# Expert stage: output summed in PSUM, next tokens gathered before the last up product, scatter in fp32r, weights split over three lanes

## The reference, cut to what matters

```python
def moe_swiglu(h, w_router, b_router, w_gate, w_up, w_down):
    B, S, D = h.shape
    ht = h.reshape(B * S, D)
    logits = (ht @ w_router).astype(jnp.float32) + b_router.astype(jnp.float32)
    top_v, top_i = lax.top_k(logits, TOP_K)
    probs = jax.nn.softmax(top_v, axis=-1)
    gates = jnp.sum(jax.nn.one_hot(top_i, N_EXPERTS, dtype=jnp.float32) * probs[..., None], axis=1)
    out = jnp.zeros((B * S, D), jnp.float32)
    for e in range(N_EXPERTS):
        a = jax.nn.silu(ht @ w_gate[e]) * (ht @ w_up[e])
        out = out + gates[:, e:e + 1] * (a @ w_down[e]).astype(jnp.float32)
    return out.astype(h.dtype).reshape(B, S, D)
```

## Time and profile before

| | |
|---|---|
| median of 3 runs | 1954.76 us (1951.22 to 1954.91) |
| the profiled execution | 1952.92 us, span 1951.0 us |
| mean granted TensorE clock | 0.972 |
| TensorE products, busy | 1840.3 us, 94% of the span |
| VectorE, busy | 1479.4 us, 76% |
| ScalarE, busy | 1105.0 us, 57% |
| bytes moved | 484.29 MB, mean 248 GB/s |

### The profile page before, as it was taken

How to read it: one execution, slowest core, us unless ns; L and a number is a source line. 1 busy time by engine, 2 the same in 40 slices (tenths; PEclk the granted TensorE clock), 3 DMA queues, 4 the chain that set the end, 5 groups by cost and what they waited for, 6 DMA issues and landing times.

```text
span 1951.0 us, 24059 instructions
## 1 busy us (share of the span) xinstructions
PE 1840.3 (94%) x8694; PEld 1519.7 (78%) x8694; DVE 1479.4 (76%) x1327; ACT 1105.0 (57%) x980; POOL 32.2 (2%) x31
## 2 busy tenths in 40 slices
PE   6999998999799999979999989989999999899898
PEld 6788886888688888767877868868778778688686
DVE  5756576455666656758979979979889799798897
ACT  3345554433334466426766757767667667576574
POOL 0001000000000200000000000000000000000000
PEclk8999999999989999979999999999999999999999
DMA  5444355554225434537979979979989899799794
GB/s 221 153 171 151 108 173 215 186 186 151 103 102 203 149 129 136 178 140 262 376 288 348 374 249 366 374 251 376 327 301 374 290 333 374 270 358 374 264 373 172
DMA packets 243931, 484.29 MB, mean 248 GB/s; under 512 B 7472, under 2 KB 11824, under 8 KB 243760
## 3 DMA queue, kind: packets, MB, share of 16 engines
q1 hardware_dynamic: 243888, 483.70, 69.1%
HBM read 482.62 MB, written 1.05 MB: 248 GB/s over the span
## 4 chain that ended last, share of the span: by engine, by line
PE 84%; DVE 7%; ACT 4%; issue 3%; DMA 1%; DVEq 0%; POOL 0%; ACTq 0%; SPq 0%; POOLq 0%
PE ps L477 26%; PE ps L478 25%; PE ps L479 25%; PE ps L482 5%; PE ps L486 3%; DVE sb_wlo L295 2%; ACT sb_whi L288 2%; DVE sb_hlo L1222 1%; DVE sb_x L1700 1%; ACT sb_hhi L1133 1%; DMA sb_ringa<-in_w_in_dram 0%; DVE sb_z L1701 0%; DVE sb_w L1205 0%; DVE sb_hlo L1221 0%; ACT sb_w L910 0%
## 5 line engine op out<-in xcount | busy, mean ns | idle before, releaser
L295 DVE TENSOR_TENSOR sb_wlo<-sb_z,sb_whi 128x2048 fp32r<-128x2048 f32 (+1 forms) x372 | 843.9, 2271 | 195.2 <-ACT sb_whi L288 191.7
L288 ACT ACTIVATE sb_whi<-sb_z 128x2048 fp32r<-128x2048 f32 (+1 forms) x372 | 706.1, 1906 | 278.4 <-PE ps L479 278.4
L477 PE MATMUL ps<-sb_whi,sb_hhi 128*128 128x512 f32 (+1 forms) x1744 | 698.8, 401 | 57.4 <-DVE sb_hlo L1222 26.9
L478 PE MATMUL ps<-sb_whi,sb_hlo 128*128 128x512 f32 (+1 forms) x1744 | 683.4, 392 | 0.0
L479 PE MATMUL ps<-sb_wlo,sb_hhi 128*128 128x512 f32 (+1 forms) x1744 | 682.8, 391 | 0.0
L477 PEld LDWEIGHTS ps<-sb_whi,sb_hhi 128*128 128x128 f32 x1744 | 334.1, 192 | 138.7 <-issue 35.6
L479 PEld LDWEIGHTS ps<-sb_wlo,sb_hhi 128*128 128x128 f32 x1744 | 333.9, 191 | 70.4
L478 PEld LDWEIGHTS ps<-sb_whi,sb_hlo 128*128 128x128 f32 x1744 | 334.2, 192 | 66.1 <-issue 1.9
L295 DVE TENSOR_TENSOR sb_wlo<-sb_ringa,sb_whi 128x2048 fp32r<-128x2048 f32 (+1 forms) x90 | 200.9, 2240 | 85.6 <-ACT sb_whi L288 85.0
L288 ACT ACTIVATE sb_whi<-sb_ringa 128x2048 fp32r<-128x2048 f32 (+1 forms) x90 | 168.5, 1877 | 155.5 <-DMA sb_ringa<-in_w_in_dram 78.8
L477 PE MATMUL ps<-sb_whi,sb_ahi 128*128 128x512 f32 x568 | 222.2, 391 | 1.0 <-DVE sb_alo L1221 1.0
(11 more groups left out here) (201 smaller groups left out, 1027.0 us busy)
## 6 DMA issues: line engine op xcount, KB each, us to landing
sb_z<-in_moe_w_gate_dram SPq DMA_DIRECT2D x112, 1024.0 KB, 5.9
sb_z<-in_moe_w_up_dram SPq DMA_DIRECT2D x112, 1024.0 KB, 6.1
sb_z<-in_moe_w_down_dram SPq DMA_DIRECT2D x112, 1024.0 KB, 5.6
sb_ringa<-in_w_in_dram SPq DMA_DIRECT2D x68, 1024.0 KB, 4.8
sb_z<-in_ffn_w_gate_dram SPq DMA_DIRECT2D x10, 1024.0 KB, 5.3
sb_z<-in_ffn_w_up_dram SPq DMA_DIRECT2D x10, 1024.0 KB, 6.4
sb_z<-in_ffn_w_down_dram SPq DMA_DIRECT2D x10, 1024.0 KB, 4.8
sb_ringa<-in_w_out_dram SPq DMA_DIRECT2D x8, 1024.0 KB, 4.9
```

What stands on the lines that cost most here:

```text
L288: nc.scalar.activation(whi[:, lane(layer, phase, s), 0:n], raw_slot(layer, phase, s)[:, 0:n], ACT.Copy).then_inc(hi_done, 1)
L295: nc.vector.tensor_tensor(wlo[:, k, 0:n], raw_slot(layer, phase, s)[:, 0:n], whi[:, k, 0:n].bitcast(F32), ALU.subtract).then_inc(split, 1)
L477: nc.tensor.matmul(out, lh, rh, start=start, stop=False)
L478: nc.tensor.matmul(out, ll, rh, start=False, stop=False)
```

## The change

- **Down product.** A down slot now holds 256 rows of the weight by all 1024 columns, instead of 512 rows by 512 columns. Banks 3 and 4 are summed over all 7 chunks in PSUM; only the first product of an item starts them. `e_sum`, `yacc` and its clearing go.
- **Output.** After the last down slot ScalarE takes both banks, times the token's gate (`gcol`), as high part `yhi` (`y_out`, 128x1024) and VectorE the low part `ylo` (`y_rest`). The gate column comes from two small products of `pick` with `gsel` in `turn_picks`, and `pickg` goes.
- **Scatter.** It is eight fp32r products (`spread` by `yhi` and by `ylo`) into banks 5, 6, 7 and 2. The first item has none.
- **Gather.** It stands after turn(5) and before up(6). The last chunk's transposes stand between the two slots of down(5). The tokens' high parts are handed to VectorE in two halves. The activations of the last chunk go to the other half of `ahi` and `alo`.
- **Order of the splits.** ScalarE does the high part of slot s+4 before `e_hi`; VectorE does `e_mult` behind the low part of slot s+6; the splits of the next item's first slots move into a function `edge`. Lanes are looked up in a table `E_LANES`, whose entries are the slot number modulo 3.
- **Loops.** Item 0 is written out ahead of the loop over items, without waiting for the number of items; the inner loop has two rounds per pass and runs twice.

```diff
+E_LANES = tuple(s % RING_L for s in range(E_SLOTS))
...
-                            return wd[bass.ds(f0, C), h * C:(h + 1) * C].rearrange("(k p) n -> p k n", p=P)
+                            return wd[bass.ds(f0 + h * (C // 2), C // 2), :].rearrange("(k p) n -> p k n", p=P)
...
+                def e_down(s, n, r, h, at=0, first=False, last=False):
                     pe.wait_ge(a_lo, n + (F_TILES + 1))
-                    pe.wait_ge(d_out, d)
-                    for h in range(2):
-                        product(1, "B", s + h, r, (3 + h,), (ahi, alo), 0, True, True)
+                    wait_lo(pe, 1, "B", s + h, r)
+                    hi, lo = (w.rearrange("p (k n) -> p k n", k=2) for w in e_lane(s + h))
+                    for half in range(2):
+                        for kk in range(2):
+                            k = 2 * h + kk
+                            m = mm3(ps[:, 3 + half, :], ahi[:, k, at:at + CAP], alo[:, k, at:at + CAP],
+                                    hi[:, kk, half * C:(half + 1) * C], lo[:, kk, half * C:(half + 1) * C],
+                                    first and k == 0, last and k == 3)
+                    m.then_inc(used, 1)
...
+                def scatter(n):
+                    pe.wait_ge(y_lo, n + 1)
                     pe.wait_ge(spread_sb, n + 1)
-                    for k, bank in enumerate((7, 3, 4, 2)):
-                        mm(ps[:, bank, :], spread[:, k // 2 * P:(k // 2 + 1) * P],
-                           yacc[:, k % 2 * C:(k % 2 + 1) * C]).then_inc(scat_mm, 1)
+                    for k, bank in enumerate((5, 6, 7, 2)):
+                        half = slice(k % 2 * C, (k % 2 + 1) * C)
+                        mm(ps[:, bank, :], spread[:, k // 2 * P:(k // 2 + 1) * P], yhi[:, half], stop=False)
+                        mm(ps[:, bank, :], spread[:, k // 2 * P:(k // 2 + 1) * P], ylo[:, half],
+                           start=False).then_inc(scat_mm, 1)
+
+                def turn_picks():
+                    for t in range(TT):
+                        mm(ps[:, 7, S:S + 1], pick[:, t, :], gsel[:, t:t + 1], start=t == 0, stop=t == 1)
+                    for t in range(TT):
+                        m = turn(ps[:, 7, t * P:(t + 1) * P], pick[:, t, :])
+                    m.then_inc(spread_t, 1)
...
 (in item(j) of TensorE, behind the rounds)
+                    s, n = E_SLOTS - 8, n0 + (E_CHUNKS - 1)
+                    e_gate(s, n, n0)
+                    e_turn(n - 1)
                     gather(j + 1)
-                    e_down(E_SLOTS - 2, n0 + (E_CHUNKS - 1), d0 + 2 * (E_CHUNKS - 1), n0)
+                    e_up(s + 2, n, n0)
+                    e_down(s + 4, n - 1, n0, 0)
+                    e_turn(n)
+                    e_down(s + 4, n - 1, n0, 1)
+                    for h in range(2):
+                        e_down(s + 6, n, n0, h, at=CAP, last=True)
...
 (ScalarE)
+                def y_out(s, r, n):
+                    wait_used(act, 1, "B", s, r)
+                    act.wait_ge(gcol_ok, n + 1)
+                    nc.scalar.activation(yhi[:, :], ps[:, 3:5, :].rearrange("p h n -> p (h n)"), ACT.Copy,
+                                         scale=gcol).then_inc(y_hi, 1)
+                def e_round(s, n, r):
+                    e_hi_of(act, s + 4, r)
+                    e_hi(n - 1)
+                    e_silu(s + 1, n, r)
+                    e_hi_of(act, s + 5, r)
...
+                def edge(j):
+                    n0 = j * E_CHUNKS + E_CHUNKS
+                    wait_used(act, 1, "B", -5, n0)
+                    gathered_hi(j + 1)
+                    e_hi_of(act, -1, n0)
+                    e_hi(n0 - 1, at=CAP)
+                    for s in range(3):
+                        e_hi_of(act, s, n0)
+                    y_out(-1, n0, j)
+                    e_hi_of(act, 3, n0)
...
 (VectorE)
+                def e_round(s, n, r):
+                    e_lo_of(dve, s + 4, r)
                     e_lo(n - 1)
+                    e_lo_of(dve, s + 5, r)
+                    e_lo_of(dve, s + 6, r)
+                    e_mult(s + 3, n, r)
...
+                def edge(j):
+                    n0 = j * E_CHUNKS + E_CHUNKS
+                    e_lo_tokens(j + 1)
+                    e_lo(n0 - 1, at=CAP)
+                    for s in range(-1, 2):
+                        e_lo_of(dve, s, n0)
+                    y_rest(j)
+                    e_lo_of(dve, 2, n0)
+                    e_lo_of(dve, 3, n0)
+                    scattered(j)
```

More of the change, by code:

```diff
@@ L75 @@
 F_SUMS = 2 * F_TILES
-E_SUMS = 2 * E_CHUNKS + 2 * TT
+E_SUMS = 2 * TT
 ROT_STEPS = 4
@@ L878, in _ @@
                     e_up(2, n0, n0)
-                    pe.wait_ge(d_out, d0)
-                    for t in range(TT):
-                        m = turn(ps[:, 7, t * P:(t + 1) * P], pickg[:, t, :])
-                    m.then_inc(spread_t, 1)
-                    with pe.Fori(0, E_CHUNKS - 1) as i:
-                        e_gate(4, n0 + i + 1, n0 + i)
-                        e_turn(n0 + i, d0)
-                        e_up(6, n0 + i + 1, n0 + i)
-                        e_down(8, n0 + i, d0 + i * 2, n0 + i)
@@ L888, in _, with e_round @@
-                    e_turn(n0 + (E_CHUNKS - 1), d0)
-                    gather(j + 1)
-                    e_down(E_SLOTS - 2, n0 + (E_CHUNKS - 1), d0 + 2 * (E_CHUNKS - 1), n0)
-                scatter(items)
+                    pe.wait_ge(d_out, j * E_SUMS + F_SUMS)
+                    turn_picks()
+                    def e_round(s, n, r, first=False):
+                        e_gate(s, n, r)
+                        e_turn(n - 1)
+                        e_up(s + 2, n, r)
+                        for h in range(2):
+                            e_down(s + 4, n - 1, r, h, first=first)
@@ L894, in _ @@
+                    e_turn(n)
+                    e_down(s + 4, n - 1, n0, 1)
+                    for h in range(2):
+                        e_down(s + 6, n, n0, h, at=CAP, last=True)
+                gather(0)
+                item(0)
+                pe.wait_ge(route_ok, 1)
+                last = pe.value_load(eid[0:1, 14:15], min_val=NE - 1, max_val=ITEMS - 1)
+                with pe.Fori(0, last) as j:
+                    item(j + 1)
+                scatter(last)
         @block.scalar
@@ L1176, in _ @@
                 with act.Fori(0, last) as j:
-                    e_rest(j)
-                    n1 = j * E_CHUNKS + E_CHUNKS
-                    wait_used(act, 1, "B", E_SLOTS - 5, j * E_CHUNKS)
-                    gathered_hi(j + 1)
-                    for s in range(3):
-                        hi_of(act, 1, "B", s, n1)
-                e_rest(last)
+                    edge(j)
+                    item(j + 1)
+                n1 = last * E_CHUNKS + E_CHUNKS
+                e_hi_of(act, -1, n1)
+                e_hi(n1 - 1, at=CAP)
+                y_out(-1, n1, last)
         @block.vector
@@ L1693, in e_lo_tokens, with y_rest @@
                     m.then_inc(gt_lo, 1)
+                def y_rest(n):
+                    dve.wait_ge(y_hi, n + 1)
+                    minus_hi(ylo[:, :], ps[:, 3:5, :].rearrange("p h n -> p (h n)"), gcol, yhi[:, :]).then_inc(y_lo, 1)
                 def scattered(n):
-                    for k, bank in enumerate((7, 3, 4, 2)):
+                    for k, bank in enumerate((5, 6, 7, 2)):
                         dve.wait_ge(scat_mm, n * 4 + k + 1)
```

210 lines of the change are left out of this document (113 added, 97 removed).

## The result

The changed kernel takes 1905.30 us (median of 4 runs, 1900.94 to 1908.13) against 1954.84 us for the kernel before on the same chip (4 runs, 1951.22 to 1955.87). The ratio is 0.9748, 95% interval 0.9723 to 0.9772. The forecast was 1909 us, in a range of 1893 to 1930, and "faster" at 0.93. The profiled execution took 1908.13 us, with a span of 1906.2.

The account below looks back on a forecast made before the run. TensorE was taken to bound the kernel, its expert-stage waits falling only between experts. Seven edges -31.5, clock -6.8, start -7.2 and end +1.5 sum to -44.0 us, from 1952.92 to 1909 us, range 1893 to 1930.

Parts of the forecast that it names:

- Scatter, -1.7 per edge: Between experts: eight fp32r products take 1.8 us of TensorE where fp32 took 3.5, gaining 1.7 us per edge.
- The chain to `ylo`: After an expert's last down slot: output copy and rest end 4.4 us on, 1.0 us before TensorE's scatter wants them.
- The tokens' stall gone, -3.2: At the next expert's first gate product: the earlier gather removes the 3.2 us wait, with over 6 us to spare.
- New stall of the transposes, +2.4: At the last chunk's transposes: TensorE waits 2.4 us for VectorE's multiply, in each of eight experts.
- Round 1, -2.4 with 0.2 left: Before an expert's round 1: the 2.62 us wait behind VectorE's adds and memset shrinks to 0.2, gaining 2.4 us.
- Sum of an edge: Per expert edge: scatter, tokens, round 1, picks and transposes together give -4.5 us; seven edges -31.5 us.
- Clock, -6.8: Behind edge stalls: eight long stalls instead of 15, half followed by low clock at 1.7 us each, gain 6.8 us.
- clock stays up: Rival: with one 2.4 us stall per expert the low clock stretches may not come at all; 1902 us, chance 0.13.
- Start and end, -7.2 and +1.5: Item 0 loses its zero scatter and stall, tokens come in halves: -7.2 us; end, with the eighth transposes' stall, +1.5.
- VectorE is late: Rival: VectorE's output copy, rest and adds at the edge run 2 us longer, costing 23 us; 1932 us, chance 0.15.
- Instruction fetch: Rival: longer loop bodies make 23 jumps wait 4.6 us each for a fetch, 106 us; 2015 us, chance 0.04.
- No change: Rival: the new order costs TensorE 0.9 us in each of 48 rounds, 43 us; 1952 us, chance 0.03.

Follow-up runs that it names:

- a first remedy: Changed kernel with VectorE's multiply of an expert's last inner half taken ahead of one of its two pieces of split weights; 1892.62 us.
- the right one: Changed kernel with the gather put just before the last transposes, and last-gate products ahead of gathered tokens on ScalarE and VectorE; 1886.68 us.

## Why the prediction was right, step by step

- **Rounds worth 0: right.** 16.82 us before, after, and with the additions put back.
- **Scatter, -1.7 per edge: right.** Eight products take 1013.66 to 1015.51, 1.85 us against 1.8 worked out. The old ones took 3.03, and the product behind them started up 0.40 late (0.63 instead of 0.23 to the next), so 3.43 and a gain of 1.6:

```profile
1283.83 3.59 PE L482 MATMUL ps<-sb_z 128*128 128x512 f32 x8
1286.86 0.79 PE L477 MATMUL ps<-sb_whi,sb_hhi 128*128 128x512 f32 x1
1287.49 0.40 PE L478 MATMUL ps<-sb_whi,sb_hlo 128*128 128x512 f32 x1
```

- **The chain to `ylo`: right.** `y_out` 1.1 us (taken 1.15), `y_rest` 1.2, spare 1.0 as forecast; the copy moved back by one split makes the scatter wait.
- **The tokens' stall gone, -3.2: right, with 8 us to spare.** The reason given, the earlier gather, was only part of it. What removes the stall is that the tokens stand ahead of the next expert's weights on VectorE. The gather alone removes nothing, the order alone removes two thirds, and an early gather on top of it the rest.
- **New stall of the transposes, +2.4: right.** 2.22 to 2.28, in all eight experts, by the row named.
- **Round 1, -2.4 with 0.2 left: right in size, half of its cause overlooked.** Nothing is left, so 2.6. The prediction puts the old wait to the four adds and the memset on VectorE. The trace has one thing more in that chain: ScalarE has a row ACT_TABLE_LOAD of 1.28 us (it loads the table of a function) ahead of an expert's first silu, and slot 3's high part stood behind that silu. It has one in each of the first seven experts and not in the last, whose gate, scatter, up products, adds and memset are the same:

```profile
L1140 ACT ACT_TABLE_LOAD  x6: 1283/1283/1283, 1017.4 to 1683.9; - x6
1829.44 0.50 PE L477 MATMUL ps<-sb_whi,sb_hhi 128*128 128x512 f32 x1 [1.66 <-DVE sb_wlo L295]
```

  (The seventh load, the first expert's, is at 884.13.) From the first gate product to the first of round 1 it is 1143.35 to 1162.74, 19.39 us, with the load and 1811.31 to 1829.44, 18.13, without, each with one low stretch in it. With the pair exchanged on VectorE it is 17.86 (1012.79 to 1030.65) and, for the last expert, 16.61 (1797.71 to 1814.32), without such a stretch. So it took 1.25 to 1.26 us of TensorE's time for a load on ScalarE. In the changed kernel the stage has one load in all, in the first expert, and slot 3's high part no longer stands behind the silu:

```profile
L1224 ACT ACT_TABLE_LOAD x1 | 1.3, 1283 | 0.0
```

  Whether item 0 written out ahead of the loop took the loads away, or the new order on ScalarE, was not tested, nor what the adds and the memset alone are worth.
- **Picks, +0.4: right.** 1020.97 to 1021.71 is 0.74, where two turns had 0.38.
- **Sum of an edge: mis-sized by 0.7.** Without low stretches a period is now 126.49. The old one, 133.47 with eight stretches in the seven (8 x 1.57 / 7 = 1.8), is 131.7 without. That is 5.2 where -4.5 was forecast, and with the clock the period is 126.90 where 128 was. Of the difference 0.4 is in the two stall terms (2.6 for 2.4 and 2.2 for 2.4), and the scatter takes 0.1 back. The other 0.4 is in the up and gate products between the old stalls: from the first gate product to the picks' end it was 15.2 us, and is 13.5. Beside scatter and picks that holds a short wait at the second up slot (it starts at 1290.16, 0.39 behind the product before instead of 0.23; VectorE's rest of that slot ends just then, behind the table load) and slower first products behind the waits (0.33 instead of 0.23). The prediction had these at nothing.
- **Clock, -6.8: mis-sized, in the direction of the rival "clock stays up".** Eight low stretches behind edges became two, six times 1.57 = 9.4 us. "About every second stall" was a rate from 15 cases and is no law: the same stall of 2.2 to 2.3 us was followed by a stretch two times in eight here and seven in eight with the fp32 scatter, and a stall of 3.2 us three times in seven in the kernel before and eight in eight with the gather moved alone. In the two versions with unchanged edges (additions put back, loop one round long) it was two in eight again. What decides it stays open, so this term rested on a rate that the runs don't bear out.
- **Start and end, -7.2 and +1.5: near.** From the first tokens' rest to the first product of round 1 it was 896.07 - 873.62 = 22.45 and is 16.71 (877.18 to 893.89): -5.7 and, with the handing over in halves (VectorE starts 1.2 behind ScalarE's copies instead of 2.2), -6.8. From the last expert's such product to the output's issue it was 117.3 (from 1829.44 to 1946.71) and is 119.6: +2.4, as the last scatter waits 2.6 for `ylo` and ends in a low stretch:

```profile
1782.25 0.50 PE L519 MATMUL ps<-sb_whi,sb_hhi 128*128 128x512 f32 x1
...
1898.02 0.50 PE L524 MATMUL ps<-sb_yhi,sb_spread 128*128 128x512 f32 x1 [2.60 <-DVE sb_ylo L1331]
...
1901.89 0.39 SPq L467 DMA_DIRECT2D out_dram<-sb_x  x1
```

- **Total.** 44.0 forecast, 44.8 between the profiled executions and 49.5 between the medians. The close hit of the first is partly luck. Between the first products of round 1 (896.07 to 1829.44, now 893.89 to 1782.25) the seven edges gave 45.0, 6.7 more than forecast, 2.6 of it clock. (The copies give 46.0; the last old wait, without its table load, was 1.0 shorter.) The start gave 6.8, the end cost 2.4, and the stage began 4.6 later in the profiled execution: 45.0 + 6.8 - 2.4 - 4.6 = 44.8. What was mis-sized at the edges and the late beginning nearly cancel.
- **Rivals.** "VectorE is late" would have needed 2 us more in its train; with the output copy 2 us later the kernel does take 21 more, so its price (23) was well taken, though part of the 21 is the wait and slow starts named there. "Instruction fetch" found no gap. "No change" fell with the 16.82.

## What to carry to other kernels

When one engine sets the time and waits only at a seam, write the seam out as a list per engine and ask for each wait which product stands in front of it as cover: taking a long step earlier can uncover another chain (the gather alone: +5.6 us), while exchanging two neighbours in the other engine's queue gave 21 us. Price the wait that comes next before you remove one; a first remedy left about half of it (1.2 of 2.2 us), the right one took the cover along. And where the start of a stage wanders by some 8 us between executions, measure the distance between two equal events inside it: it repeated to some 0.01 us between three kernels whose edges were alike and which had two low stretches each (126.90, 126.90, 126.91). And compare the pass that is unlike the others: the last expert had no table load, and so priced it.

## What the runs showed of the hardware

- Stalls of TensorE of 0.9, 1.2 and 1.6 us at the edges (28 cases in four of the versions) were never followed at once by the lower clock level; those of 2.2 to 2.3 us were, two times in eight in the changed kernel and seven in eight with the fp32 scatter, at the same length of stall. A stretch of 3.4 us costs 1.57 us; the other one of the changed kernel, between 1252.52 and 1380.64, costs 1.6. What decides whether it comes stays open.
- A table load on ScalarE takes 1.28 us and cost TensorE 1.25 to 1.26 where it stood in the chain that TensorE waited for.
- Eight passes of fp32 products of 128x512 take 3.03 us and the product behind them 0.40 more to get going; eight fp32r products of the same shape take 1.85.
- The loads of the expert weights land 7.0 us after their issue, where it was 5.6, with rows of twice the length in the down loads. No wait came of it. Whether the row length or the closer spacing of the requests does it was not tested; the gate's loads, whose form is unchanged, went from 5.9 to 6.9 too.
- In the rounds the DMA engines' busy share reads full, in the kernel before (1.02 from 940 to 990 us) as after. The changed kernel's window:

```profile
940.00:990.00 50.00, 50.00 (x244) 42.03 (x243) 42.84 (x24) 34.57 (x23) 0.00 (x0) 1.00 1.00 372
```

So the share of the DMA engines reads 1.00 while TensorE never waits, and SyncE still waits 679 of the 900 us from 1000 to 1900 for VectorE to free a raw slot. Whether a faster TensorE in the rounds would find the loads in its way, no run here tried.
